# A new order of the Recurrence on all five engines: eight gate blocks per tile, and the key norm's sum in the second gate block of the next tile

## The reference

```python
def rwkv_branch(cur, prev, state0, g, mix, w0, w_up, a0, a_up, k_k, k_a, r_k, gn_g, gn_b):
    xs = cur + (prev - cur) * mix
    r, k, v, wd, ad = jnp.split(xs, ...)
    w = -jax.nn.softplus(-(w0 + jnp.tanh(wd) @ w_up)) - 0.5
    decay = jnp.exp(-jnp.exp(w))
    a = jax.nn.sigmoid(a0 + ad @ a_up)
    kk = heads(k * k_k)
    kk = kk * lax.rsqrt(jnp.maximum(jnp.sum(kk * kk, axis=-1, keepdims=True), 1e-24))
    k = k * (1.0 + (a - 1.0) * k_a)
    ...
    for each token:
        S = S * w_t + (S @ -kk_t) (kk_t * a_t)^T + v_t k_t^T
        y = S @ r_t
    y = group norm of y per head, times gain, plus bias, plus (sum(r * k * r_k)) * v
    return y * silu(g), S
```

## Time and profile before

| | us |
|---|---|
| runs of the kernel | 1642.64, 1643.59, 1644.87; median 1643.59 |
| the profiled execution | span 1640.3 (the page gives no other time for it) |
| tiles 0 to 14 of the Recurrence (887.43 to 1347.46 of the span) | 460.03 |
| one steady tile (tile 7, 1135.40 to 1165.45) | 30.05 |
| tile 15 (1347.46 to 1382.57) | 35.11 |
| ACT's table load in tile 16 | 1.28 |

### The profile page before, as it was taken

The page is one execution under the profiler, slowest core; times in us unless marked ns, Lnnn a source line. Parts: engine busy times, 40 slices in busy tenths (PEclk is TensorE's granted clock), DMA queues, the critical chain, the costliest instruction groups (busy, mean ns, idle before and its releaser), DMA issues. The chain is left out here.

```text
span 1640.3 us, 46809 instructions
## 1 busy us (share of the span) xinstructions
PE 1591.8 (97%) x20218; PEld 1301.9 (79%) x20218; DVE 806.8 (49%) x1153; ACT 879.3 (54%) x1833; POOL 498.8 (30%) x354
## 2 busy tenths in 40 slices
PE   8999999999999899999998999999999997999999
PEld 7788888888888788899986777777777876777787
DVE  4344544454445531121226677667677677544432
ACT  6466566656665631222237777777777776224320
POOL 1423221222121012221223456455556456400000
PEclk9999999999999999999999999999999999999999
DMA  6323211122113543433353232232232236286652
GB/s 244 88 82 94 70 51 61 55 73 61 60 43 116 196 134 123 135 105 106 114 174 125 70 93 79 73 93 69 83 87 89 81 97 206 70 318 225 206 173 77
DMA packets 136302, 184.43 MB, mean 112 GB/s; under 512 B 59153, under 2 KB 88337, under 8 KB 135842
## 3 DMA queue, kind: packets, MB, share of 16 engines
q1 hardware_dynamic: 129186, 170.83, 32.3%
q10 hardware_dynamic: 6912, 10.62, 1.8%
HBM read 122.42 MB, written 59.55 MB: 111 GB/s over the span
## 5 line engine op out<-in xcount | busy, mean ns | idle before, releaser
L681 PE MATMUL a_ps_proj<-a_w_hi,a_x_hi 128*128 128x512 f32 x384 | 157.6, 410 | 2.5 <-ACT a_qk L431 1.4
L681 PE MATMUL a_ps_proj<-a_w_hi,a_x_lo 128*128 128x512 f32 x384 | 151.6, 395 | 0.0
L681 PE MATMUL a_ps_proj<-a_w_lo,a_x_hi 128*128 128x512 f32 x384 | 151.1, 393 | 0.0
L584 DVE SCALAR_TENSOR_TENSOR a_stage<-a_ps_s,a_new_bias 128x256 f32<-128x256 f32 x64 | 27.2, 425 | 241.5 <-PE a_ps_s L708 235.8
L2529 PE MATMUL r_ps_gate<-gate_w_hi,gate_x_hi 128*128 128x512 f32 x272 | 119.2, 438 | 5.2 <-PEq L66 3.4
L1187 DVE SCALAR_TENSOR_TENSOR j_out<-j_ps,j_rest,j_part 128x512 f32<-128x512 f32 (+2 forms) x45 | 29.0, 644 | 184.0 <-ACT j_last_cols L1131 139.1
L2529 PE MATMUL r_ps_gate<-gate_w_lo,gate_x_hi 128*128 128x512 f32 x272 | 111.6, 410 | 0.0
L360 POOL TENSOR_TENSOR a_xT<-a_xT,a_row 128x1024 f32<-128x1024 f32 x17 | 40.4, 2374 | 228.2 <-DMA a_row<-scratch_rstd 220.0
L469 ACT ACTIVATE a_stage<-a_stage,a_small 128x640 f32<-128x640 f32 (+4 forms) x128 | 95.8, 751 | 1.5 <-DVE a_small L592 1.5
L1061 POOL TENSOR_TENSOR j_v_prev<-j_v_prev,shift_x 128x512 f32<-128x512 f32 x17 | 22.2, 1307 | 228.3 <-DMA j_v_prev<-scratch_v_raw 216.7
L1129 ACT ACTIVATE j_part<-j_last_cols,j_shift_in 128x1 f32<-128x1 f32 x45 | 13.2, 294 | 141.7 <-PE j_ps L1220 141.7
(11 more groups left out here) (414 smaller groups left out, 4677.6 us busy)
## 6 DMA issues: line engine op xcount, KB each, us to landing
a_xT<-in_x_T SPq DMA_DIRECT2D x17, 512.0 KB, 3.4
scratch_xT<-a_xT SPq DMA_DIRECT2D x17, 512.0 KB, 2.6
raw<-scratch_xT SPq DMA_DIRECT2D x17, 512.0 KB, 4.8
scratch_gates<-r_gate_out SPq DMA_DIRECT2D x34, 256.0 KB, 2.4
z_gate<-scratch_gates SPq DMA_DIRECT2D x17, 512.0 KB, 4.6
a_x<-in_x_prompt SPq DMA_DIRECT2D x16, 512.0 KB, 3.6
o_x<-in_x_prompt SPq DMA_DIRECT2D x14, 512.0 KB, 4.9
out_y_prompt<-o_y SPq DMA_DIRECT2D x14, 512.0 KB, 2.9
```

The lines of the kernel that those rows point to most:

```text
L584: nc.vector.scalar_tensor_tensor(out=out[:, :, OLD:WIN], in0=ps_new, scalar=SCALE, in1=new_bias[:, 2 * c:2 * c + 2, :], op0=ALU.mult, op1= ...
L681: mm = nc.tensor.matmul(ps_proj[:], a[n % 2][:, k, :], w[:, k, g * AW:(g + 1) * AW], start=(k == 0 and i == 0), stop=(k == KT - 1 and i == 2))
```

## The change

All keys of the Recurrence get new values. `LEVEL_AT` is now a table with a key for each of a level's five steps, and the chunks' steps have tables of their own; tile 16 (mode "s") keeps the old values in most of them. The gates come in 8 blocks in place of 10. The key norm's sum, `key_sums`, is a function of its own: for tiles from 1 on it is called in PE's `front` at key 3, one tile later than before, where it came at key 29 of `mix`. No product and no elementwise operation is added or taken away. The core of the diff:

```diff
-        LEVEL_AT, CHAIN_AT = 4.1, (20.5, 26.85)
-        GRAM_AT = (25.05, 28.15)
+        LEVEL_AT = {"p": ((0, 0.3, 2.4, 3.2, 4.4), (4.2, 5.2, 6.35, 7.1, 7.8), (7.8, 9, 10.15, 10.9, 11.5), (11.6, 12.8, 14.8, 15.6, 16.2),
+                          (16.4, 17.4, 18.6, 19.4)),
+                    "s": tuple(tuple(4.1 * l + x for x in (0, 1.2, 2.1, 3.2, 4)) for l in range(3))}
+        LEVEL_W, LEVEL_MASK, LEVEL_Z, LEVEL_COPY, LEVEL_TURN = range(5)
+        STATE_AT, SOLVE_AT = {"p": (19.1, 24.2), "s": (20.5, 26.85)}, {"p": (20.9, 25.3), "s": (22.9, 28.75)}
+        RHS_AT, U_AT = {"p": (19.9, 24.9), "s": (21.2, 27.55)}, {"p": (21.6, 26), "s": (23.7, 30)}
+        U_USED_AT, READ_AT = {"p": (22.4, 26.8), "s": (24.5, 30.9)}, {"p": (23.8, 27.5), "s": (26.2, 32.4)}
+        GRAM_AT, GRAM_MASK_AT = (19.8, 22.9), (20.7, 24)
...
-        GATE_BLOCKS = (((1.1, 5), (3.2, 5), (5.2, 5), (7.3, 5), (9.3, 4)), ((13.4, 4), (17.5, 4), (19.6, 4), (23.6, 4), (28.9, 8)))
+        GATE_BLOCKS = (((0.2, 9), (3.3, 2), (4.8, 6), (8.4, 7)), ((12.2, 11), (16.9, 7), (21.5, 3), (25.9, 3)))
...
# SyncE: loads of xs
-                yield 24.7
+                yield 12
                 past(sp, t - 1, "rhat")
                 load_xs(t, u, slice(0, 4), r_loaded)
...
# GpSimd, tail
-                yield 8.8
+                yield 4
                 was_read(pool, t, "bonus")
...
-                yield 18
+                yield 9.1
                 need(pool, t, "y_rstd", "y_centred")
...
-                yield 18.1
+                yield 10.2
                 need(pool, t, "y_scaled")
...
# ScalarE, tail
-                yield 4
+                yield 2.4
                 need(act, t, "y_centred")
...
-                yield 8.3
+                yield 4.6
                 need(act, t, "y_var")
...
# VectorE, front
-                    yield 1.3
+                    yield 3.8
                     bound_norm(t)
-                yield 6.3
+                yield 6.5
                 need(dve, t, "rnorm", "kk")
...
# VectorE, tail
                 if mode == "p":
-                    yield 14.7
+                    yield 5.8
                     decay_state(t, u, 1)
...
# TensorE, mix and front
-                yield 29
+                if t == 0:
+                    yield 29
+                    key_sums(t)
+
+            def key_sums(t):
                 pe.wait_ge(head_sums_ready, 1)
                 need(pe, t, "kk_hi", "kk_lo")
                 ps, done = free_bank(t, "kk_sum")
...
             def front(t, u, mode):
-                yield 11.5
+                if t > 0:
+                    yield 3
+                    key_sums(t)
+                yield 6.9
                 pe.wait_ge(shared.consts_loaded, 16)
...
-                yield 21.8
+                yield 15.4
                 need(pe, t, "kt", "bt")
                 turn_two(t, "b_tok", c4(bt[:]), "k_tok", c4(kt[:]))
...
# TensorE, back
-                    yield LEVEL_AT * l
+                    yield LEVEL_AT[mode][l][LEVEL_W]
...
-                    yield at + 2.4 if n == 0 else GRAM_AT[1] + 0.6
+                    yield SOLVE_AT[mode][n]
```

More of the change, by code:

```diff
@@ L1628, in gates @@
                         load_gate_x(t + 1)
-                        yield 24.6
+                        yield 22.2
                         sp.wait_ge(u_ready, 2 * t - 1)
@@ L1665, in front @@
             def front(t, u, mode):
-                yield 12
+                yield 10.5
                 if 0 < t < DEC:
@@ L1712, in mix @@
             def mix(t, u, mode):
-                yield 13
+                yield 12.1
                 arrived(pool, t, u)
@@ L1723, in mix @@
                     return
-                yield 21.6
+                yield 16
                 need(pool, t, "kk", "acc")
@@ L1815, in gates @@
                 if t < DEC:
-                    yield 33.7
+                    yield 26.9
                     split_x(t + 1)
@@ L1845, in mix @@
             def mix(t, u, mode):
-                yield 12.5
+                yield 8.5
                 if t > 0:
@@ L1852, in mix @@
                 if t == 0:
-                    yield 13.5
+                    yield 9.5
                     square_keys(t)
-                yield 16.6
+                yield 12.4
                 ps, read = written(act, t, "decay")
@@ L1860, in mix @@
                 last.then_inc(read, 1)
-                yield 18.2
+                yield 13.4
                 ps, read = written(act, t, "iclr")
@@ L1867, in mix @@
                 if t > 0:
-                    yield 21.7
+                    yield 17.5
                     square_keys(t)
-                    yield 27.7
+                    yield 21.9
                 was_read(act, t, "iclr")
@@ L1890, in front @@
                 if t > 0:
-                    yield 3.4
+                    yield 5
                     norm_root(t)
-                yield 9.5
+                yield 10.1
                 wait(act, ready["ps_y"], t - 1)
@@ L1900, in front @@
                     if name == "k_tok":
-                        yield 14
                         ps, read = written(act, t, "bonus")
                         nc.scalar.activation(bonus[u][:], ps[:, 0:2 * UNITS].rearrange("p (m o) -> p m o", o=2)[:, :, 0], ACT.Copy).then_inc(read, 1)
-                    yield {"k_tok": 22.9, "b_tok": 24.1}[name]
+                    yield {"k_tok": 17, "b_tok": 18}[name]
                     ps, read = written(act, t, name)
                     nc.scalar.activation(buf[u][:].rearrange("p m d -> p (m d)"), ps[:], ACT.Copy).then_inc(read, 1)
-                yield 31.3
+                yield 26.6
                 need(act, t, "z2")
@@ L1923, in back @@
                 l = LEVELS[mode] - 1
-                yield LEVEL_AT * l + 3.2
+                yield LEVEL_AT[mode][l][LEVEL_COPY]
                 act.wait_ge(q_written, LP * t + l + 1)
@@ L1975, in gates @@
             def gates(t, u, mode):
-                yield 11.3
+                yield 10.25
                 copy_gates(t, 0)
                 if t < DEC:
-                    yield 26
+                    yield 23.4
                     split_x(t + 1)
@@ L1990, in gates @@
                         split_w(k)
-                yield 32.5
+                yield 27.4
                 copy_gates(t, 1)
@@ L2066, in mix @@
                     return
-                yield 20.4
+                yield 14.7
                 was_read(dve, t, "decay")
@@ L2102, in front @@
                 scaled(u, 0, c4(kk_n[:]), True, mode).then_inc(ready["ahat"], 1)
-                yield 10.4
+                yield 9.6
                 r_arrived(dve, t, u)
                 scaled(u, 1, xs[u][:, 0:4], False, mode).then_inc(ready["rhat"], 1)
-                yield 13.6
+                yield 13.4
                 need(dve, t, "bmul", "inv_g")
@@ L2110, in front @@
                                                op1=ALU.mult).then_inc(ready["bt"], 1)
-                yield 17.7
+                yield 14
                 need(dve, t, "kmod")
@@ L2120, in front @@
                 for name, out, n in (("B0", bm, 0), ("K0", km, 0), ("B1", bm, 1), ("K1", km, 1)):
-                    yield GRAM_AT[n] + 1.2
+                    yield GRAM_MASK_AT[n] + (0.7 if out is km else 0)
                     ps, read = written(dve, t, name)
@@ L2125, in front @@
                     if name == "K1":
-                        yield 31.2
+                        yield 25.9
                         need(dve, t, "a_eye")
@@ L2156, in back @@
                     for n in range(NCH):
-                        yield (25.3, 31.7)[n]
+                        yield (23.1, 27.5)[n]
                         dve.wait_ge(s_written, 2 * t + n + 1)
@@ L2164, in back @@
                 else:
-                    yield LEVEL_AT * 3
+                    yield 12.3
                     need(dve, t, "ahat", "rhat")
@@ L2191, in tail @@
             def tail(t, u, mode):
-                yield 2
+                yield 1
                 need(dve, t, "ps_y")
@@ L2308, in mix @@
             def mix(t, u, mode):
-                yield 15.5
+                yield 10.7
                 if t == 0:
@@ L2478, in back @@
                 for n in range(NCH):
-                    at = CHAIN_AT[n]
-                    yield at
+                    yield STATE_AT[mode][n]
                     if mode == "p":
@@ L2500, in back @@
                     solve(n)
-                    yield (24.5, 30.9)[n]
+                    yield U_USED_AT[mode][n]
                     pe.wait_ge(u_ready, 2 * t + n + 1)
@@ L2508, in back @@
                         last.then_inc(s_written, 1)
-                    yield (26.2, 32.4)[n]
+                    yield READ_AT[mode][n]
                     last = read_out(n)
```

40 lines of the change are left out of this document (20 added, 20 removed).

## The result

The changed kernel takes 1620.97 us (median of 4 runs, 1617.77 to 1623.00), the kernel before 1643.29 (4 runs, 1642.64 to 1644.87) in the comparison: a ratio of 0.987, 95% interval 0.9851 to 0.989. It is 22.3 us faster, where the prediction gave 9.6 and a range that ended at 1627. The direction was right, the size was not.

What follows compares the result with a forecast made beforehand. PE's instruction stream was taken to bound the kernel. Per steady tile -0.40 - 0.18 - 0.26 + 0.20 = -0.64 us, -9.6 over 15 intervals, edges 0: 1643.59 to 1634.0 us, range 1627 to 1641.

Steps and rivals of the forecast that it cites:

- What bounds the kernel: PE's own instruction stream sets a tile's pace: PE busy for 29.85 of tile 7's 30.05 us.
- Switches: PE's moves between gate and small products: 10 blocks become 8 at 0.20 us each, -0.40 us a tile.
- third rival: The 0.20 us belongs to small products' data, so fewer blocks save nothing: -3.6 us in all, 1640.0; chance 0.08.
- Level 3's cover: PE's wait for DVE's mask ahead of level 3's Z goes, covered by more gate products: -0.18 us a tile.
- The chunks: Tile's end on PE: wait before the second chunk's grams goes, -0.26 us; new wait before the second solve, +0.20.
- The steady tile: Sum of the terms for one tile: -0.64 us, 30.05 becomes 29.41; -9.6 us for the 15 intervals.
- The surplus: Time of the 15-tile window beyond 15 steady tiles: 9.3 us, kept as is; bounds 0 and about double.
- first rival: PE's "issue" stalls before 64x64 products in tiles 0 to 14 all go: 4.4 us less, 1629.6; chance 0.13.
- second rival: DVE late at level 2, its decay and ahat lengthened beside POOL operations: slower, 1647.5 us; chance 0.08.
- Edges: Tile 15 gains up to 4.5 us, tile 16 loses 4.5 to 5.5 (table loads, splits, silu): 0, from -3 to +4.
- The sum: Whole kernel: 1643.59 - 9.6 + 0 = 1634.0 us.

Runs made afterwards that it cites:

- ten_blocks: Changed kernel with ten gate blocks in place of eight, same number of products: 1627.95 us, smallest tile 29.64 us.
- before_nine: Kernel before with level 4's gate block joined to the one ahead (nine blocks) and a fifth product in level 3's block: 1639.52 us, ratio 0.9986.
- gram_late: Changed kernel with the second chunk's gram products back between y_state and the second solve: 1694.48 us, ratio 1.032.
- act_tail15: Changed kernel with ACT's y_sq, logarithm and exponential for tile 15's norm at their old keys in tile 16: 1620.94 us, ratio 0.9882.
- all_tail15: Changed kernel with old keys in tile 16 for ACT's and also DVE's tile-15 operations (y_sum, y_var, state decay): 1618.56 us, repeated 1620.31 us.

## Why the prediction was wrong in size

- **What bounds the kernel.** Right: PE's stream sets the pace, and each change of it by an edit showed in the tile.
- **Switches.** The step that failed: the term of -0.40 us. It priced a block at 0.20 us, from the start of a block's first product, and took "whatever its size" as the whole price. The small products ahead of a block also take 0.10 to 0.11 us longer, which the slope of three block sizes can't show, since that cost lies ahead of the first start. With 0.31, two blocks are worth 0.61 (ten_blocks) and not 0.40: 0.2 us a tile, 3 us in all. The third rival is refuted by the same run. This term alone would have left the forecast at 1630.8, still above the measured time; the other parts of the miss follow.
- **Level 3's cover** (headed level 2's in the prediction, where the text rightly spoke of level 3). Right in kind, and short by 0.05: besides the 0.18 ahead of Z, level 3's Z took 0.67 where one ahead of a block takes 0.62 or 0.63, and it falls to 0.63 in before_nine, where the mask is covered. The gates fell by 0.64, for 0.40 + 0.18 in the sum.
- **The chunks.** Right to 0.05: -0.11 us for -0.26 + 0.20, and the new wait came out at 0.19. What the sum missed is that this step carries the others, as gram_late shows.
- **The steady tile.** -1.02 for -0.64. Of the 0.38 missed, 0.22 is the entry of two blocks (Z groups of 0.62 that became 0.52), 0.05 level 3's Z, 0.05 the chunks and 0.06 the gates.
- **The surplus.** Kept by the prediction; 5.0 to 7.1 in profiles of the changed kernel, 7.9 and 9.3 before. The first rival, that the stalls called "issue" go, happened at most in part: in the lists of waits they come to 4.6 and 3.8 us in the two profiles before, to 2.7, 3.5 and 2.0 in the three after, now ahead of W, of the solve and of gate products. What they are stays open; no run tested it.
- **Level 2 and DVE (second rival).** It didn't come: the longest decay is 0.59 us, and the wait of PE for a mask at that level isn't in the list of waits. The rival took the long duration to the new place, though my own schedule had POOL idle there. Its price doesn't follow from its figures either: a decay longer by 1.07 us against a cover of 0.5 would be 0.6 late and not 0.13.
- **Edges.** Forecast 0, from -3 to +4. Tile 15 gave 3.2 us and the start of the Recurrence 1.7, which I had not looked at; tile 16 to the end cost 6.8: +2.0 in sum, in the range. The reason given for tile 16 bears most of it, by its trace: the loads with their two operations fill 3.1 of the 4.1 us by which level 1's copy is later, and PE's wait for the copy has the lower clock behind it. Its price of 4.5 to 5.5 us fits the 5.6 us by which level 2's Z is later. act_tail15 gave only 1.7 when they were taken away, but that kernel made a wait of its own (y_var, 2.16 us), so it doesn't price the loads. What the prediction did not see is DVE's y_sum and y_centred ahead of level 0's mask, 1.3 of the 4.4 us that both engines' old keys win (all_tail15). The start of the Recurrence varies by itself: 27.7 to 30.0 us in the seven profiles with the changed order, 30.9 and 31.0 before, so not all of the 1.7 is the change's.
- **The sum** by its own terms is -15.3 - 2.3 + 2.0 = -15.6 us between the two profiles, inside the changed phase, for -9.6. 4.3 us more lie ahead of the Recurrence and are the granted clock of two executions: luck, and no work of the change. 2.4 us lie between the difference of the spans and that of the medians (22.3). The clock stands behind part of that gap as well: its median is 0.989 over the 41 runs of the kernel before beside the experiments, 0.991 over the 12 of the changed one, and 0.002 of 1640 us is 3.3 us, as an estimate. Why the changed program should get more of it stays open, and so do the last few us. The range was too narrow because the price of a block had been read from one side only and given no upper bound, and because the clock, the surplus and the starts of the phases were taken as fixed.

## What to carry to other kernels

Price a switch between kinds of instruction from the last instruction of one kind that is undisturbed to the first undisturbed one of the next, and so on both sides; a slope over block sizes gives the far side alone. A block that seems only to cost may be covering somebody's inputs: compare the moment when they are ready with the start of what needs them, since a hidden wait shows as no idle time (0.36 us from ACT's last copy to PE in three kernels, 0.81 in the one that had slack). Keys of a hand-written order are tied in pairs across engines, producer and reader: put back one of them and the queue of the other waits. And before two profiles are compared by a phase, lay the same instructions side by side: a distance that jumps where the granted clock differs, and is constant elsewhere, isn't the change's.

## What was not expected of the hardware

In gram_late a wait of 2.6 us on PE was followed, after 0.1 to 1.6 us of full work, by a stretch at the lower clock in 12 of tiles 1 to 14, though PE was busy all through it (in tile 6 it made nine gate products 1.04 us longer); two tiles with the same wait were spared, and 1.5 us shorter. A logarithm and the exponential behind it needed two table loads, 1.28 us each, when they stood ahead of the kernel's own load of their common set, and none behind it. And single runs of the kernel before, in one series, lay up to 13 us apart (1635.85 to 1648.54), with the smallest tile constant to 0.02 us; the time goes with the granted clock, 1648.54 us at 0.985 and 1636.38 at 0.995 at the two ends of 41 runs.
